# Moving the large work area of a two-layer block from 1,984 to 0 bytes past a multiple of 2,048

## The reference, cut to what matters

```
def reference(x, ...):
    # first block: dilated attention + Mamba-2, gated; feed-forward 4096 wide
    u = rmsnorm(x, norm_mix_pre_w)
    q, k, v, z, xbc, dt_raw, gate_logits = split(u @ w_in)
    att = dilated_attention(q, k, v) @ w_att_proj
    ssm = mamba2_mixer(z, xbc, dt_raw, ...) @ w_ssm_proj
    h = x + rmsnorm((g_att * att + g_ssm * ssm) @ w_out, norm_mix_post_w)
    f = square(relu(rmsnorm(h, norm_ffn_pre_w) @ w_up)) @ w_down
    x = h + rmsnorm(f, norm_ffn_post_w)
    # second block: 31-tap convolution + retention; gated feed-forward 2816 wide; embedding gate
    u = rmsnorm(x) @ w_in_2
    x = x + rmsnorm(concat(conformer_conv(u), retention(u)) @ w_out_2)
    h = rmsnorm(x)
    x = x + rmsnorm((silu(h @ w_ffn_gate_2) * (h @ w_ffn_up_2)) @ w_ffn_down_2)
    return x + rmsnorm(sigmoid(x @ w_ple_gate_2) * (p_2 @ w_ple_proj_2))
```

## The kernel before, in words

| moving operand | stage | address past a multiple of 128 | of 2,048 | 512-token triples | 256-token triples |
|---|---|---|---|---|---|
| `u_hi`, `u_lo` | all inputs of a layer or feed-forward part, `ple_gate` | 0 | 128 | the rest | 192 |
| `att_hi`, `att_lo` | attention projection | 64 | 1,984 | 48 | 0 |
| `y_hi`, `y_lo` | Mamba projection | 64 | 1,984 | 128 | 0 |
| `mix_hi`, `mix_lo` | first `w_out`; the last four chunks of `mix_lo` lie in `s_hi`'s place, at 128 | 64 | 1,984 | 40 | 48 |
| `v_hi`, `v_lo` | `w_down` of the first layer, `w_out_2` | 64 | 1,984 | 272 | 96 |
| `h_hi`, `h_lo` | `w_ffn_down_2` | 64 | 1,984 | 176 | 0 |

## Time and profile before

### The profile page before, as it was taken

One profiled execution on the slowest core, in us unless ns is written; L12 is line 12 of the kernel. 1 busy time (PEld: TensorE's weight loads), 2 busy tenths in 40 slices (PEclk: granted clock), 3 DMA queues, 4 the chain that ended last, 5 costly groups with the idle time before them and its releaser, 6 DMA issues.

```text
span 1832.0 us, 25027 instructions
## 1 busy us (share of the span) xinstructions
PE 1784.7 (97%) x9040; PEld 1469.4 (80%) x9040; DVE 838.8 (46%) x1577; ACT 755.6 (41%) x1244; POOL 767.5 (42%) x590
## 2 busy tenths in 40 slices
PE   7999999999999999999999999899999999999997
PEld 5777788888888888888888888777778888888877
DVE  4554546677676211272111124898747433320044
ACT  5444554566664322352323233523355323222253
POOL 4322344433334455345444444343333444445543
PEclk9999999999999999999999999999999999999998
DMA  5212233332333322233232322122112323233321
GB/s 191 69 57 89 70 105 110 108 104 92 104 100 120 103 92 92 81 127 103 93 103 92 103 92 92 62 89 69 58 58 73 101 92 103 92 103 104 103 81 46
DMA packets 47802, 170.67 MB, mean 93 GB/s; under 512 B 5312, under 2 KB 7488, under 8 KB 47456
## 3 DMA queue, kind: packets, MB, share of 16 engines
q1 hardware_dynamic: 44352, 156.25, 25.9%
q10 hardware_dynamic: 3360, 13.17, 2.1%
HBM read 167.24 MB, written 2.16 MB: 92 GB/s over the span
## 4 chain that ended last, share of the span: by engine, by line
PE 91%; DVE 7%; ACT 1%; issue 1%; DMA 0%; DVEq 0%; SPq 0%; POOLq 0%; POOL 0%; ACTq 0%
PE bank L394 27%; PE bank L396 27%; PE bank L395 27%; DVE bank L2350 2%; PE bank L573 1%; PE bank L718 1%; PE bank L582 1%; PE bank L595 1%; DVE xs L1864 1%; PE bank L722 1%; PE bank L702 1%; DVE u_lo L1869 1%; PE bank L432 1%; PE bank L693 0%; PE bank L671 0%
## 5 line engine op out<-in xcount | busy, mean ns | idle before, releaser
L367 POOL TENSOR_TENSOR w_lo<-raw,w_hi 128x512 fp32r<-128x512 f32 x578 | 760.6, 1338 | 1037.4 <-ACT w_hi L992 1037.2
L394 PE MATMUL bank<-u_hi,w_hi 128*128 128x512 f32 (+1 forms) x1624 | 628.0, 387 | 16.8 <-DVE glu L2330 7.5
L396 PE MATMUL bank<-u_hi,w_lo 128*128 128x512 f32 (+1 forms) x1624 | 614.7, 379 | 0.0
L395 PE MATMUL bank<-u_lo,w_hi 128*128 128x512 f32 (+1 forms) x1624 | 614.3, 378 | 0.0
L992 ACT ACTIVATE w_hi<-raw 128x1024 fp32r<-128x1024 f32 x289 | 303.8, 1052 | 287.7 <-PE bank L396 287.5
L394 PEld LDWEIGHTS bank<-u_hi,w_hi 128*128 128x128 f32 x1624 | 307.3, 189 | 78.7 <-issue 13.6
L396 PEld LDWEIGHTS bank<-u_hi,w_lo 128*128 128x128 f32 x1624 | 307.0, 189 | 58.3
L395 PEld LDWEIGHTS bank<-u_lo,w_hi 128*128 128x128 f32 x1624 | 307.6, 189 | 53.7 <-issue 0.2
L394 PE MATMUL bank<-v_hi,w_hi 128*128 128x512 f32 (+1 forms) x368 | 134.6, 366 | 1.7 <-ACT y_u L1607 0.9
L396 PE MATMUL bank<-v_hi,w_lo 128*128 128x512 f32 (+1 forms) x368 | 133.4, 362 | 0.0
L395 PE MATMUL bank<-v_lo,w_hi 128*128 128x512 f32 (+1 forms) x368 | 132.4, 360 | 0.0
(11 more groups left out here) (320 smaller groups left out, 2162.7 us busy)
## 6 DMA issues: line engine op xcount, KB each, us to landing
raw<-weights SPq DMA_DIRECT2D x289, 512.0 KB, 3.3
bc<-acs ACTq DMA_DIRECT2D x16, 512.0 KB, 3.8
xs<-x SPq DMA_DIRECT2D x4, 512.0 KB, 5.4
xs<-x ACTq DMA_DIRECT2D x1, 2048.0 KB, 7.7
rt<-ret_tables ACTq DMA_DIRECT2D x1, 1536.0 KB, 6.3
out<-xs SPq DMA_DIRECT2D x12, 128.0 KB, 1.8
dist<-att_tables SPq DMA_DIRECT2D x1, 512.0 KB, 10.7
p_raw<-p ACTq DMA_DIRECT2D x1, 512.0 KB, 7.2
```

The lines of the kernel that those rows point to most:

```text
L367: return nc.gpsimd.tensor_tensor(w_lo[:, slot, w], raw[:, slot, w], w_hi[:, slot, w].bitcast(F32), ALU.subtract)
L394: mm(dst, w_hi[:, slot, w], hi, start=first, stop=False)
L395: mm(dst, w_hi[:, slot, w], lo, start=False, stop=False)
L396: return mm(dst, w_lo[:, slot, w], hi, start=False, stop=last)
```

## The change

`work` is rounded up to a multiple of 128 bytes. This moves it 64 bytes on, from 135,104 to 135,168, which is 66 times 2,048. All tensors that are placed from `work` move by 64 bytes with it, `v_at`, `g_at`, `m_at` and `t_at` included. The tensors below `work` stay where they were; among them are all weights, `u_hi`, `u_lo`, `xs`, `s_hi`, `s_lo`, the upper half of `mix_lo`, `tiny`, `diag` and `sq`. `h_scale` leaves the end of the work area and goes 1,536 bytes into `cst`, over the permutation, the slopes and most of `heads_t`. The number of instructions, their order on each engine and their waits are the same in both programs.

```diff
@@ -195,6 +195,7 @@
     s_lo = place("s_lo", [P, 2, T], F32R)
     vec = place("vec", [P, NVEC])
     half = place("half", [P, 32])
+    cst_at = top[0]
     cst = place("cst", [P, 4 * P + N_HEADS])
     heads_t = place("heads_t", [P, 3, QB, S_HEADS])
     tiny = place("tiny", [P, 64])
@@ -203,7 +204,7 @@
     ident, ones, tri, perm = (cst[:, k * P:(k + 1) * P] for k in range(4))
     slopes = cst[:, 4 * P:4 * P + N_HEADS]
     y_u = place("y_u", [P, C8, T], at=u_at)
-    work = top[0]
+    work = (top[0] + 127) // 128 * 128
     K = 1024
 
 
@@ -271,7 +272,7 @@
     h_hi = place("h_hi", [P, H2, T], F32R, at=work)
     h_lo = place("h_lo", [P, H2, T], F32R, at=work + 44 * K)
     h_tmp = place("h_tmp", [P, T], at=work + 88 * K)
-    h_scale = place("h_scale", [P, T], at=work + 90 * K)
+    h_scale = place("h_scale", [P, T], at=cst_at + 4 * 3 * P)
     pj = place("pj", [P, C8, T], at=work)
     ple_tanh = place("ple_tanh", [P, 2, T], at=t_at)
```

## The result

The changed kernel takes 1840.26 us, the median of six runs from 1839.11 to 1840.66. The kernel before took 1832.6 us in the six runs beside it, 1829.64 to 1835.5. The ratio is 1.0040, with the 95% interval 1.0028 to 1.0051. So the change costs some 7.5 us, where the forecast said that it gains 3.8. The time lies outside the predicted range, and within 1.5 us of the rival that had the smallest chance (1841.7 us).

A forecast was written before the change was run, and what follows sets the result against it. It took TensorE's matmuls, one after the other, to bound the kernel. Terms 4.0 + 0.55 + 0.4 + 0.3 - 1.4 = 3.8 us less gave 1830.3, for the median 1829.6 us; range 1823 to 1834.5 us (8 in 10).

The forecast's parts named there:

- Whole triples of the work area fall to the pace of `u`: 624 triples of 512 tokens over `att`, `y`, `v`, `h`: each 6.4 ns faster, 4.0 us gained.
- the 0.55 us that `mix` was to gain: 40 whole triples over `mix`: 20 gain 8 ns each and 20 gain 20 ns, 0.55 us.
- the new one is worse: Rival, chance 0.08: work area at 0 against weights at 128 makes whole triples take 0.700 us; 1841.7 us.
- new and better: Rival, chance 0.10: the work area's new position to the weights beats the pace of `u`; down to 1815 us, halfway 1822.
- Triples of 256 tokens: Short triples over `v` (both tails) and `mix` slow to the 0.360 us of `u`: 1.4 us lost.
- Going over between kinds: First triples behind `u`, and returns from `y` to `u`, lose their extra time: 0.4 and 0.3 us gained.
- The signs: Trace over `h_hi`: 389 ns and 119.0 us for 176 triples if right; 394 address not cause, 397 or more position.
- What cost nothing: Factors' new place and VectorE at moved addresses taken as 0, at most 0.7 and 2 us; weight stream not starving TensorE.
- The size of the forecast's own case: All work-area triples at the pace of `u`: 3.8 us gained, 1829.6 us, chance 0.64.
- The rule weighed: Skill's rule that TensorE has two read ports and never waits; by it addresses do not matter, change worth 0.

The follow-up runs named there:

- third kernel: Changed kernel with everything moved by 64 bytes, the work area by 192 in all, so weights, `u` and work area lie at 192 modulo 2,048: 1828.07 us.
- second kernel: Changed kernel with the work area another 128 bytes on, at 128 modulo 2,048 like the weights and `u`: 1827.99 us.

## Why the prediction was wrong

**"Whole triples of the work area fall to the pace of `u`"** is the step that failed. It took the common offset of `y`, `att`, `v` and `h`, 64 past a multiple of 128, as what made them slow. But in the trace of before these four had a second thing in common, a distance of -192 to the weights, against 0 for `u`. No row of before parted the two; the third kernel of the experiments did, and showed that the offset alone costs nothing. The term was 4.0 us gained. It is 7.6 us lost, and the 0.55 us that `mix` was to gain did not come.

**The rival "the new one is worse"** is what happened. Its price came from the right row: `mix_hi` against `mix_lo`'s upper half, 0.700 us, and 0.700 us is what `h` and `v` show now. Its sum, 1841.7 us, is 1.4 above the median measured. A part of that closeness is luck: it starts 0.8 us above the six runs' median of before, takes 8.3 us for whole triples and `mix` where the starts show 7.6, and leaves out the 0.9 us of the short ones. Its chance, 0.08, was too small, and the text had the reason in hand: it said that a distance counts at most modulo 512 and leaves a shift of 128 open, and that rows 7 show that one operand's place to the next counts. The only good place known was that of `u`, at distance 0 from the weights, and this spoke for the distance at least as much as for the address. The rival "new and better" fell; no distance beats 0 for whole triples with 128-column tiles.

**Triples of 256 tokens** were right in direction: in the later tail of `v` they went from 0.340 to 0.360 us as forecast, in the earlier one from 0.353 to 0.356 instead of 0.360, and over `mix` they did not change. The loss was 0.9 us against 1.4.

**Going over between kinds.** In the changed kernel two kinds stayed; the first four triples back on `u` behind `y` take 644.05 - 641.31 = 2.74 us there, 2.77 before. The second kernel has one kind, and there the extra is gone: the first triple over `h` behind `u` takes 0.680 us, and the first four back on `u` behind `y` take 2.72 us. This step was right for the case that it assumed.

**The signs.** One sign that the prediction gave pointed the wrong way. It said that a duration of 394 ns for the line over `h_hi` would mean that the address is not the cause, and 397 or more that the position to the weights is. The median stayed at 394, with the position as the cause. Its other sign, the time from the first start to the last, told the truth: neither 119.0 nor 120.1 us, but 122.5.

**What cost nothing** was right: the factors' new place (ratio 1.0009 alone), VectorE at other starts (739 to 756 ns again) and the weight stream. GpSimd's wait, 1037.2 us in the earlier trace rows, is now:

```profile
POOL w_lo L368 <- ACT w_hi L993: 1044.6, 273, 23.7
```

It has grown by 7.4 us, about as the span has (6.4): it fills up whatever TensorE takes.

**The size of the forecast's own case** was about right. Once all lie alike, as in the second and third kernel, whole triples take 0.680 us, and the kernel takes 4.9 to 5.0 us less than before (4.2 with the work area at 384), where the forecast's sum was 3.8. Starts compared one by one, the second kernel gains 4.4 us over the whole triples with their entries (forecast 4.0 and 0.4), 0.4 over `mix` (0.55) and 0.5 at the returns to `u` (0.3), and loses 1.3 over the short triples (1.4).

**The rule weighed.** The Trainium skill ("SBUF — State Buffer", Who interferes with whom) says that TensorE never waits on anyone and has two independent read ports, one for the moving operand and one for the weight load. The first half agrees with the runs: the paces with nothing else running are those of the full kernel. By the second half all distances would cost the same, and they take 680 to 700 ns, and 712 at a start 4 bytes off. The measurement decides: the pace of TensorE's matmuls depends, by up to 5%, on how its own two operands lie to each other. What inside the chip makes it so stays open.

## What to carry to other kernels

When operands of one matmul go at two paces, look at how they lie to each other and not only at where each lies; for stationary tiles of 128 columns and moving rows of 512, the moving operand wants to start a multiple of 256 bytes from the stationary one, for every pair of a group. For other sizes another distance was best here, so measure it. A gain of this kind, 0.25%, is smaller than the scatter that goes with the granted clock (0.4%), so compare runs at equal clock, or the starts of the same matmuls one by one. Before moving a whole area, find a row that parts "its address" from "its distance", or give both the same chance. And read the pace from starts over a count, since the modelled durations kept their median at 394 ns while the pace went from 686 to 700.

## What the runs showed of the hardware

- With 128 by 128 tiles and 512 columns, three matmuls take 680, 687, 698 or 700 ns as the moving operand starts 0, 64, 128 or 192 bytes past the weights, modulo 256, and 712 ns at 4 bytes. The weights' own address (0, 64, 128 and 256 tried) does not count. Two paces exist here too: distance 64 gave 687 ns, and 700 with weights at 128 and the moving operand at 1,984.
- With 256 columns the order is another: 360, 353, 356, 340 ns. The place that is best for long matmuls is the worst of these four for short ones.
- One layout can hold two steady paces, 340 or 353 ns, by what ran before.
- Fewer stationary columns (32 for 128) shorten the weight load from 188 to 108 ns and do not shorten the matmul's pace; they shrink what the distance costs from 20 to 4 ns a triple, and another distance is best.
- Spans of one kernel follow the mean granted clock: 1826.7 us at 0.994 and 1834.5 us at 0.990.
- VectorE, by contrast, takes 739 to 756 ns over 120 starts at 4-byte steps, before and after.
